# One staging slot fewer and reordered side work in a two-block transformer kernel

## The reference, cut to what matters

```python
def first_block(x, ...):
    for l in range(2):
        x = layer_norm(ALPHA * x + 0.5 * swiglu(x, ffn1_w13[l], ffn1_w2[l]), ln_g[l, 0], ln_b[l, 0])
        m = mixer(x, w_in[l], ...)            # gated linear recurrence (hgrn2) and a gated spatial branch
        x = layer_norm(ALPHA * x + m, ln_g[l, 1], ln_b[l, 1])
        x = layer_norm(ALPHA * x + 0.5 * swiglu(x, ffn2_w13[l], ffn2_w2[l]), ln_g[l, 2], ln_b[l, 2])
def swiglu(x, w13, w2):                       # w13: 1024 x 5632, w2: 2816 x 1024
    a, b = jnp.split(x @ w13, 2, axis=-1)
    return (jax.nn.silu(a) * b) @ w2
# second block, per layer: RMS norm, swiglu_2; token_mixer (dilated window attention with 8 heads,
# and a two-directional mLSTM with 4 heads); swiglu_2; each with a norm before and after
```

## Time and profile before

| | |
|---|---|
| median of 3 runs | 2117.06 us (2116.61 to 2117.34) |
| the profiled execution: own time | 2117.34 us |
| its span, first to last instruction | 2115.6 us |
| PE busy | 2092.5 us, 99% |
| DVE busy | 1661.3 us, 79% |
| ACT busy | 1082.5 us, 51% |
| POOL busy | 80.1 us, 4% |
| DMA | 395.55 MB, mean 187 GB/s |

### The profile page before, as it was taken

The page is one execution under the profiler, slowest core; times in us unless marked ns, Lnnn a source line. Parts: engine busy times, 40 slices in busy tenths (PEclk is TensorE's granted clock), DMA queues, the critical chain, the costliest instruction groups (busy, mean ns, idle before and its releaser), DMA issues.

```text
span 2115.6 us, 28773 instructions
## 1 busy us (share of the span) xinstructions
PE 2092.5 (99%) x10566; PEld 1775.3 (84%) x10566; DVE 1661.3 (79%) x3046; ACT 1082.5 (51%) x1568; POOL 80.1 (4%) x128
## 2 busy tenths in 40 slices
PE   8999999999999999999999999999999999999998
PEld 7887999888788799988878887988888888888886
DVE  6888766888878877778888887778888888678886
ACT  5445553544544455444454446575445445666443
POOL 0000010000000000000000001010000000101000
PEclk9999999999999999999999999999999999999999
DMA  7765755666576584556647767346665665645662
GB/s 254 238 190 169 223 164 161 188 215 193 171 218 196 172 236 139 188 167 226 193 155 211 217 190 200 119 138 207 212 196 179 211 194 164 184 140 174 205 191 89
DMA packets 314367, 395.55 MB, mean 187 GB/s; under 512 B 17972, under 2 KB 272212, under 8 KB 313972
## 3 DMA queue, kind: packets, MB, share of 16 engines
q1 hardware_dynamic: 309120, 375.52, 57.9%
q0 software_dynamic: 4944, 18.14, 2.7%
q10 hardware_dynamic: 164, 0.06, 0.0%
HBM read 392.59 MB, written 1.06 MB: 186 GB/s over the span
## 4 chain that ended last, share of the span: by engine, by line
PE 94%; DVE 4%; ACT 1%; issue 1%; POOL 0%; DMA 0%; SPq 0%; DVEq 0%; POOLq 0%; ACTq 0%
PE bank L308 26%; PE bank L310 26%; PE bank L309 26%; PE bank L302 4%; PE bank L303 4%; PE bank L304 4%; DVE w_lo L292 1%; PE bank L477 1%; DVE hidden L463 1%; PE bank L1441 1%; PE bank L1462 1%; PE bank L971 1%; PE bank L1533 1%; ACT w_hi L285 0%; DVE x L775 0%
## 5 line engine op out<-in xcount | busy, mean ns | idle before, releaser
L285 ACT ACTIVATE w_hi<-stage 128x1024 fp32r<-128x1024 f32 x711 | 746.6, 1058 | 642.0 <-PE bank L310 557.4
L292 DVE TENSOR_TENSOR w_lo<-stage,w_hi 128x1024 fp32r<-128x1024 f32 x711 | 865.1, 1224 | 227.9 <-ACT w_hi L285 220.2
L308 PE MATMUL bank<-w_hi,xt_hi 128*128 128x512 f32 x1760 | 692.8, 394 | 0.6 <-DVE xt_lo L815 0.4
L310 PE MATMUL bank<-w_hi,xt_lo 128*128 128x512 f32 x1760 | 686.0, 390 | 0.0
L309 PE MATMUL bank<-w_lo,xt_hi 128*128 128x512 f32 x1760 | 685.7, 390 | 0.0
L308 PEld LDWEIGHTS bank<-w_hi,xt_hi 128*128 128x128 f32 x1760 | 331.0, 188 | 69.2 <-issue 1.2
L310 PEld LDWEIGHTS bank<-w_hi,xt_lo 128*128 128x128 f32 x1760 | 330.6, 188 | 69.2
L309 PEld LDWEIGHTS bank<-w_lo,xt_hi 128*128 128x128 f32 x1760 | 331.1, 188 | 66.2
L463 DVE STREAM_TRANSPOSE hidden<-hidden 32x128 f32<-32x128 f32 (+1 forms) x1264 | 365.2, 289 | 19.7
L308 PE MATMUL bank<-w_hi,mt_hi 128*128 128x512 f32 x768 | 303.9, 396 | 6.7 <-DVE mt_lo L545 6.7
L310 PE MATMUL bank<-w_hi,mt_lo 128*128 128x512 f32 x768 | 299.5, 390 | 0.0
(11 more groups left out here) (275 smaller groups left out, 1401.7 us busy)
## 6 DMA issues: line engine op xcount, KB each, us to landing
stage<-in_ffn_w SPq DMA_DIRECT2D x352, 256.0 KB, 3.2
stage<-in_ffn_w_in SPq DMA_DIRECT2D x352, 256.0 KB, 3.1
stage<-in_ffn_w SPq DMA_DIRECT2D x88, 512.0 KB, 3.7
stage<-in_ffn_w_out SPq DMA_DIRECT2D x88, 512.0 KB, 3.7
stage<-in_w_in SPq DMA_DIRECT2D x80, 512.0 KB, 4.3
stage<-in_mix_w_in SPq DMA_DIRECT2D x56, 512.0 KB, 4.0
stage<-in_w_out SPq DMA_DIRECT2D x16, 512.0 KB, 4.8
stage<-in_mix_w_out SPq DMA_DIRECT2D x16, 512.0 KB, 3.5
```

Of the source, the lines that this page charges most:

```text
L285: act.activation(w_hi[:, u % RING, :], stage[:, u % STAGED, :], ACT.Copy).then_inc(S["hi_ready"], 1)
L292: dve.tensor_tensor(w_lo[:, u % RING, :], stage[:, u % STAGED, :], f32(w_hi[:, u % RING, :]), ALU.subtract).then_inc(S["lo_ready"], 1)
L308: pe.matmul(o, m_hi, hi, start=first, stop=False)
L310: return pe.matmul(o, m_lo, hi, start=False, stop=last)
```

## The change

- `STAGED` goes from 5 to 4. The freed place holds a fixed row of ones (`ones8`, set once at the start) and `g_neg1`, which replaces the row in `gm`.
- ffn stages: the first block turns go from two units (v = 8, 9) to one (v = 7), and within a unit they come after the gates. At the end `dve_norm_var` comes ahead of the last gate of tile 1.
- mix1: one more `w_lo` comes ahead of the product of queries and forget gates.
- mix2: the bounds are made at head 0, right behind the scans, and not at head 1; `conv_in(3)` comes behind the units of head 4. At the end ACT makes all units up to 40 (five of the next stage) ahead of `act_norm_sq`, and DVE makes one `w_lo` between the variance and `dve_norm_x`.
- POOL loads the rows without waiting for the 30 units or for the sigmoid.
- the small steps for the lower bounds count on a semaphore of their own (`lb_step`), and DVE waits for the ones once, at its start.

PE's instructions stand in the same order in both kernels.

```diff
-STAGED = 5
+STAGED = 4
...
+        g_neg1 = sb("g_neg1", [2 * H, T])
+        ones8 = sb("ones8", [2 * H, T])
...
-        ones8 = gm[0:2 * H, 1, 0:T]
-        g_neg_rows = hidden_flat[0:2 * H, 768:768 + T], gm[0:2 * H, 0, 0:T]
+        g_neg_rows = hidden_flat[0:2 * H, 768:768 + T], g_neg1[:, :]
...
         def block_turns(s):
-            first = [(8, 2, 10, [(0, 1)])] if s else [(16, 2, 18, [(0, 2)])]
+            first = [(7, 1, 9, [(0, 1)])] if s else [(16, 2, 18, [(0, 2)])]
...
         def dve_ffn(dve, s):
...
-                for v0, length, _, tiles in block_turns(s):
-                    if v0 <= v < v0 + length:
-                        for a in range(4 * (v - v0) // length, 4 * (v - v0 + 1) // length):
-                            dve_turn_blocks(dve, s, tiles, a)
                 for i in range(STEPS):
...
+                for v0, length, _, tiles in block_turns(s):
+                    if v0 <= v < v0 + length:
+                        for a in range(4 * (v - v0) // length, 4 * (v - v0 + 1) // length):
+                            dve_turn_blocks(dve, s, tiles, a)
             dve_norm_start(dve, s, 0)
+            dve_norm_var(dve, s, 0)
             dve_gate(dve, s, 1, STEPS - 1)
-            dve_norm_var(dve, s, 0)
             dve_norm_x(dve, s, 0)
...
         def dve_mix1(dve, s, L):
-            lo_upto(dve, base + 24)
+            lo_upto(dve, base + 25)
             dve.wait_ge(S["hg_q"], at("hg_q", L, 1))
...
         def pool_mix1(pool, s, L):
             pool_hold(pool, S["x_ready"], x_done(s - 1, 1))
-            pool_hold(pool, S["hg_sig"], at("hg_sig", L))
...
         def act_mix2(act, s, L):
             merged_hi(3)
-            hi_upto(act, b + 38)
+            hi_upto(act, b + 40)
+            hi_upto(act, b + 41)
             act_norm_sq(act, s, 0)
-            hi_upto(act, b + 40)
             act_xt(act, s + 1, 0)
-            hi_upto(act, b + 41)
             act_pre_sq(act, s + 1, 0)
...
         def dve_mix2(dve, s, L):
                 dve.tensor_tensor_scan(g_cum_rows[1][rev], ones8[:, :], g_lf_row[rev], 0.0, ALU.mult, ALU.add)\
                    .then_inc(S["g_scan"], 1)
-
-            def gate_bounds():
-                rev = (slice(None), slice(None, None, -1))
                 for d in range(2):
...
                 if h == 4:
                     conv_in(2)
-                    conv_in(3)
                 lo_upto(dve, base + units_by_head(h) + RING)
                 if h == 0:
                     gate_rows()
                 if h == 1:
                     conv_in(0)
-                    gate_bounds()
...
                 if h == 4:
+                    conv_in(3)
                     conv_taps(1, (3, 4))
...
             dve_norm_var(dve, s, 0)
+            lo_upto(dve, base + 39)
             dve_norm_x(dve, s, 0)
...
         def pool_mix2(pool, s, L):
-            pool.memset(ones8, 1.0).then_inc(S["margins"], 1)
...
             pool.memset(neg_half[:, :], -0.5).then_inc(S["ones_set"], 1)
+            pool.memset(ones8[:, :], 1.0).then_inc(S["ones_set"], 1)
...
                 elif 0 < s <= BLOCK2:
                     pool_hold(pool, S["x_ready"], x_done(s - 1, 1))
-                    pool_hold(pool, S["hi_ready"], FIRST[s] + 3 * RING)
                     load_rows(pool, s)
                 elif s > BLOCK2:
                     pool_hold(pool, S["pre_x"], pre_at(s, 1, 1))
-                    pool_hold(pool, S["hi_ready"], FIRST[s] + 3 * RING)
                     load_rows(pool, s)
...
         def _(dve):
+            dve.wait_ge(S["ones_set"], 2)
```

More of the change, by code:

```diff
@@ L87 @@
     zb_out=2, ya=1, yb=2, y_sum=2, y_hi=2, y_lo=2,
-    margins=7, mixrows2=32, wg_in=16, wg_hi=1, wg_lo=1,
+    margins=6, mixrows2=32, wg_in=16, wg_hi=1, wg_lo=1,
     aqk0_done=1, aqk_out=2, rot=12, a_turned=2, a_t_out=8, av_out=2, srow_out=2,
@@ L112, in build @@
         for n in ("hi_ready", "lo_ready", "used", "x_in0", "x_in1", "x_rest", "first_half", "const_in", "rest_in", "ones_set", "tables_in",
-                  "tables_turned", "tables_out", "x_out", "held", "rows_in",
+                  "tables_turned", "tables_out", "lb_step", "x_out", "held", "rows_in",
                   "gu_done0", "silu0", "silu1", "gated0", "gated1", "h_turned", "h_blocks",
@@ L844, in act_lower_bounds @@
         def act_lower_bounds(act):
-            act.wait_ge(S["tables_out"], 6)
-            act.activation(lb_tmp[:, 3:5, :], lb_tmp[:, 1:3, :], ACT.Exp).then_inc(S["tables_out"], 1)
+            act.wait_ge(S["lb_step"], 3)
+            act.activation(lb_tmp[:, 3:5, :], lb_tmp[:, 1:3, :], ACT.Exp).then_inc(S["lb_step"], 1)
         def dve_tables(dve):
@@ L856, in dve_tables @@
             mx = lb_tmp[:, 0, :]
-            dve.tensor_tensor(mx, lbr_tab[:, 0, :], lbr_tab[:, 1, :], ALU.max).then_inc(S["tables_out"], 1)
-            dve.wait_ge(S["tables_out"], 4)
+            dve.tensor_tensor(mx, lbr_tab[:, 0, :], lbr_tab[:, 1, :], ALU.max).then_inc(S["lb_step"], 1)
+            dve.wait_ge(S["lb_step"], 1)
             for l in range(2):
-                dve.tensor_tensor(lb_tmp[:, 1 + l, :], lbr_tab[:, l, :], mx, ALU.subtract).then_inc(S["tables_out"], 1)
+                dve.tensor_tensor(lb_tmp[:, 1 + l, :], lbr_tab[:, l, :], mx, ALU.subtract).then_inc(S["lb_step"], 1)
         def dve_lower_bounds(dve):
             mx, e = lb_tmp[:, 0, :], lb_tmp[:, 3:5, :]
[L864 to L873, removed]
+            dve.wait_ge(S["lb_step"], 4)
+            dve.tensor_tensor(lb_tmp[:, 5, :], e[:, 0, :], e[:, 1, :], ALU.add).then_inc(S["lb_step"], 1)
+            dve.wait_ge(S["lb_step"], 5)
+            dve.reciprocal(mx, lb_tmp[:, 5, :]).then_inc(S["lb_step"], 1)
+            dve.wait_ge(S["lb_step"], 6)
+            dve.tensor_tensor(lb_tab[:, 1, :], e[:, 1, :], mx, ALU.mult).then_inc(S["lb_step"], 1)
+            dve.memset(lb_tab[:, 0, :], 0.0).then_inc(S["lb_step"], 1)
+            dve.wait_ge(S["lb_step"], 8)
+            dve.tensor_scalar(om_tab, lb_tab, -1.0, 1.0, ALU.mult, ALU.add).then_inc(S["lb_step"], 1)
+            dve.wait_ge(S["lb_step"], 9)
         def w_cols(w, c0, n, k0=0, nk=KD):
@@ L1791, in gate_rows @@
                 dve.wait_ge(S["g_rows"], at("g_rows", L))
-                dve.wait_ge(S["margins"], at("margins", L, 1))
                 rev = (slice(None), slice(None, None, -1))
-                dve.tensor_tensor_scan(g_cum_rows[0], ones8, g_lf_row, 0.0, ALU.mult, ALU.add)\
+                dve.tensor_tensor_scan(g_cum_rows[0], ones8[:, :], g_lf_row, 0.0, ALU.mult, ALU.add)\
                    .then_inc(S["g_scan"], 1)
-                dve.tensor_tensor_scan(g_cum_rows[1][rev], ones8, g_lf_row[rev], 0.0, ALU.mult, ALU.add)\
+                dve.tensor_tensor_scan(g_cum_rows[1][rev], ones8[:, :], g_lf_row[rev], 0.0, ALU.mult, ALU.add)\
                    .then_inc(S["g_scan"], 1)
-            def gate_bounds():
-                rev = (slice(None), slice(None, None, -1))
                 for d in range(2):
@@ L1808, in gate_bounds @@
                     dve.wait_ge(S["g_scan"], at("g_scan", L, d + 3))
-                    dve.tensor_tensor_scan(o, ones8, a, -1e30, ALU.mult, ALU.max).then_inc(S["g_scan"], 1)
+                    dve.tensor_tensor_scan(o, ones8[:, :], a, -1e30, ALU.mult, ALU.max).then_inc(S["g_scan"], 1)
                 for d in range(2):
@@ L1982, in pool_mix2 @@
             pool.memset(va[:, :, :, P:P + 1], 1.0).then_inc(S["margins"], 1)
+            pool.wait_ge(S["margins"], at("margins", L, 3))
+            pool.memset(q_odd_parts[1][0:64], 0.0).then_inc(S["margins"], 1)
             pool.wait_ge(S["margins"], at("margins", L, 4))
-            pool.memset(q_odd_parts[1][0:64], 0.0).then_inc(S["margins"], 1)
-            pool.wait_ge(S["margins"], at("margins", L, 5))
             pool.wait_ge(S["x_turned"], xt_at(s, 1, 1))
             pool.memset(aqk_t[64:P, 0:4, :], 0.0).then_inc(S["margins"], 1)
-            pool.wait_ge(S["margins"], at("margins", L, 6))
+            pool.wait_ge(S["margins"], at("margins", L, 5))
             pool.wait_ge(S["rot"], at("rot", L))
@@ L2040, in _ @@
             pool.memset(neg_half[:, :], -0.5).then_inc(S["ones_set"], 1)
+            pool.memset(ones8[:, :], 1.0).then_inc(S["ones_set"], 1)
             pool.wait_ge(S["hi_ready"], 3 * RING)
             pool.dma_start(const[:, P:], A["shape_constants"][:, P:]).then_inc(S["rest_in"], 16)
-            pool.wait_ge(S["ones_set"], 1)
+            pool.wait_ge(S["ones_set"], 2)
             load_rows(pool, 0)
```

## The result

The changed kernel takes 2128.09 us (2126.98 to 2129.0, 5 runs) against 2116.74 (2116.51 to 2117.34, 5 runs): a ratio of 1.0052, 95% interval 1.0038 to 1.0065. It is slower by some 11 us, where 1.6 were forecast; the time lies outside the range. The profiled spans are 2126.7 and 2115.6, so 11.1 us have a place in the traces.

The account below looks back on a forecast made before the run. PE was taken to bound the kernel, in unchanged order, so only its waits could change: -2.2 - 4.1 + 6.8 + 1.1 = +1.6 us, giving 2118.7 against the median. The 8-in-10 range was 2112.5 to 2123.5.

Parts of the forecast that it names:

- What bounds the kernel: PE, busy 99% of the span, sets the time; the weights are ahead and wait for PE to free a place.
- the exchange: At eight ffn stage ends, variance ahead of the last gate: gain 2.2 us in block 1, 4.1 in block 2.
- The mix2 end: At two mix2 ends, weight copies ahead of the squares make PE wait for `xh`: 6.8 us lost, bounds 1.8 to 8.6.
- stands in the 0.74 gap for POOL's power and sticks out 0.45: At the mix2 end, DVE's new `w_lo` of about 1.2 us fits mostly into an existing gap, adding 0.45.
- PE waits 3.4, twice 6.8: At each of two mix2 ends PE waits 3.2 us for `xh` and about 0.2 for its second half.
- The mix2 heads: In two mix2 stages, earlier bounds and later `conv_in(3)` cost 0.55 us each stage, 1.1 together (0.4 to 1.9).
- 0.2 to 0.25 is lost: At mix2 head 1, bounds of 2.90 us now precede its masks, with 2.71 us in hand.
- Loads that starve: Rival: with four slots and rows loading beside weights, PE waits at 11 stage starts, +5.5 us, 2124.2; chance 0.14.
- edits at nothing: Block turns, mix1's extra `w_lo`, the wait for ones, unheld rows and one slot less were priced at no cost.
- the ring: Ten units of weights, taken as full, were to hide the earlier row loads and the later loads from one slot less.
- The squares are not held: Rival: b + 40 lands early at the mix2 ends, so gains stay, 5.2 to 3.4 us faster; chance 0.13.
- the exchange gives half: Rival: waits for silu or bank hold `norm_x` at ffn ends, gain only 3.1 us, 2121.9; chance 0.13.

Follow-up runs that it names:

- the first experiment: The kernel before with one edit, the variance ahead of the last gate at the end of each ffn stage: 2110.11 us, ratio 0.9967, 6.6 us faster.

## Why the prediction was wrong

- **What bounds the kernel, and the exchange: right.** The gains were forecast as 2.2 and 4.1 and are 2.4 and 4.3, and alone, in the first experiment, 6.6. Reading a stall as next start minus last start minus 0.227, and following the chain behind it until the next thing is late, gave each end to within 0.1 us.
- **The mix2 end: the mechanism right, the price too low.** ACT waits for the landing of b + 40, whose load waits for `w_lo` of b + 36, as forecast. The waits of PE are 4.10 and 4.27 and not 3.4 (and 1.2 comes back when `xh` of tile 1 comes, which the sum didn't have either). Two terms were mis-sized. From the end of that `w_lo` (1411.46 and half of 2.35, so 1412.7) to the last copy at 1417.80 it took 5.1 us and not 4.6: the second half, issued at 1413.12, landed at 1417.78, 4.7 us later and not 3.7, with loads of the units on either side in flight (its issue came 0.3 sooner behind the `w_lo` than assumed). From the squares to the first half of `xh` it took 5.3 (1418.77 to 1423.38 + 0.65) and not 4.95, since POOL's power took 1.47 us and not 0.56: my step "stands in the 0.74 gap for POOL's power and sticks out 0.45" took the two engines as independent, and they are not (without that `w_lo` the power took 0.56).
- **The step that failed is one the sum did not have:** "PE waits 3.4, twice 6.8" ended the count when PE restarts. It restarts at the lower clock, or falls to it just behind the restart: 2.56 and 1.69 us more, 4.2 together in the profiled execution. This is the largest of the terms that were off. A wait of the forecast 3.4 us would most likely have brought it too: in the kernel without that `w_lo`, with waits of 3.0 and 3.6, the clock fell at both ends.
- **The mix2 heads: too low, 1.1 against 3.3 (3.6 with 0.3 at the stage's start).** Each part was priced at its first wait. The bounds cost 0.53 at the first turn in either stage, where my step said "0.2 to 0.25 is lost", then 0.34 at the turns behind it, which it left out; that these are one chain through the masks and exponentials is read from the order and wasn't tried apart. `conv_in(3)` cost 0.77, just over the end of its bounds, where I took 0.3 with no row for it.
- **Loads that starve: this rival was partly right.** I gave it 5.5 us at eleven starts with half a microsecond each. It came at two places with 2.8 in all, beside 1.5 MB of rows where I took some 1 MB; one of the places doesn't come in every execution. The kernel with four slots alone takes the time of the kernel before, and the one with unheld rows that of the exchange alone; it is where both are in that PE waits. I had listed both under "edits at nothing" with one cover, the ring, and had not added their claims on it.
- **The squares are not held, the exchange gives half: both fell**, by the trace after and by the first experiment.
- The measured sum is 9.5 over the forecast: 4.2 of the clock, 2.8 of the weights, 2.5 of the heads, 1.6 of the waits for `xh`, less 1.2 given back and 0.4 more of gain. The range left out that the terms could all be at their upper ends together (+7.4 by my own bounds), with a cost outside the bounds on top.

## What to carry to other kernels

Ask of each move what it lets begin sooner and what it puts behind a wait: the small variance ahead of a gate that waits anyway gave 6.6 us for nothing, while copies whose data had not landed, put ahead of the squares, cost 11 (with four slots and the `w_lo`; 4 without these). If you forecast that PE waits several microseconds in one piece, look up what its clock does behind such a wait in the traces you have, and count the restart too. Two edits that are each free because the same buffer covers them must be priced together.

## What the runs showed of the hardware

- **The clock behind a wait of PE.** In the changed kernel, after waits of 4.1 and 4.3 us, the granted clock was 0.50 (1.2 GHz) over the next 5.2 us at the first end and 0.54 over 3.6 us at the second. After waits of 3.0 and 3.6 us (no `w_lo` there) it was 0.64 on average over 4.8 us. After 1.3 and 2.7 us (two copies ahead) it stayed at 1.00 in the traced execution, but the mean clock and the times of five further executions of nine say that it most likely fell in these. Nothing here tells what in these stretches decides it.
- **DVE holds up POOL.** The power of 128 numbers on POOL takes 0.55 to 0.56 us alone, and 1.47 beside a `w_lo` on DVE (1.21 us, from 1420.33 to 1421.54). The Trainium skill ("SBUF — State Buffer", "Who interferes with whom") has the rule: a DVE instruction with two inputs in SBUF contends with a POOL instruction that reads SBUF, by an exclusive lock and not by sharing. The trace agrees, since the power ended 0.42 after the `w_lo` did, and without that `w_lo` it took 0.56.
- **Two queues.** Beside 1.5 MB on POOL's queue the median landing of a 256 KB load was 7.1 us with four slots and 6.9 with five; in the same stretch (920 to 928 us) without the rows it was 3.5.
